# Byte 64 for every stationary operand, byte 0 for every moving one

## The reference

```python
# first block, per layer
px = modulate(rms_norm(x, g1), sh1, sc1) @ w_in        # same for ctx
mix_x = concat([latent_attention(qx, k_all, v_all), fourier_mix(fx),
                chunk_spatial_gate(ux, gvx, v_g, w_s, b_s)]) @ w_out
x = x + gt1 * mix_x
x = x + gt2 * square(relu(modulate(rms_norm(x, g2), sh2, sc2) @ w1)) @ w2
# second block, per layer
proj = rms_norm(x, attn_norm_g) @ w_in_2               # 3656 columns
mix = concat([moba(...), diff(...), dsa(...)])         # three attentions
x = x + mix @ w_out_2
h2 = rms_norm(x, ffn_norm_g)
x = x + (silu(h2 @ w_gate_2) * (h2 @ w_up_2)) @ w_down_2
```

## The kernel before

| stage | stationary | moving | columns | matmuls | stationary byte before | after |
|---|---|---|---|---|---|---|
| rows1, layers 0 and 1 | act | w | 512 / 256 | 432 / 48 | 0 | 64 |
| out1, layers 0 and 1 | act | w | 512 | 288 | 0 | 64 |
| up1, layer 0 | w | act | 512 / 256 | 672 / 192 | 0 | 64 |
| up1, layer 1 | w | act | 256 | 768 | 64 | 64 |
| down of MLP 1, layers 0 and 1 | hid1 | w | 512 | 1152 | 0 | 64 |
| rows2 and out2, both layers | act | w | 512 / 328 / 256 | 768 / 96 / 96 | 0 | 64 |
| up2, both layers | w | act | 256 | 2112 | 64 | 64 |
| down of MLP 2, both layers | hid2 | w | 512 | 528 | 0 | 64 |

## Time and profile before

### The profile page before, as it was taken

The page is one execution under the profiler, slowest core; times in us unless marked ns, Lnnn a source line. Parts: engine busy times, 40 slices in busy tenths (PEclk is TensorE's granted clock), DMA queues, the critical chain, the costliest instruction groups (busy, mean ns, idle before and its releaser), DMA issues.

```text
span 1592.6 us, 23486 instructions
## 1 busy us (share of the span) xinstructions
PE 1541.2 (97%) x9164; PEld 1262.6 (79%) x9164; DVE 1028.4 (65%) x1577; ACT 795.5 (50%) x1356; POOL 114.2 (7%) x130
## 2 busy tenths in 40 slices
PE   6999999999999999998999999999999999999999
PEld 2864689778888887567898878779998787689987
DVE  3637756455456437576785576978995558879973
ACT  3537735343345225565664456645554456555542
POOL 0111000010001000100000031010000111000000
PEclk9999999999999999999999999999999999999999
DMA  9528623487568524586998689436665596356653
GB/s 360 152 84 313 215 75 114 145 264 253 162 220 277 162 66 133 176 279 190 335 319 300 211 272 312 160 108 183 191 197 191 184 326 227 106 141 192 198 190 115
DMA packets 201005, 322.41 MB, mean 202 GB/s; under 512 B 14576, under 2 KB 100864, under 8 KB 200768
## 3 DMA queue, kind: packets, MB, share of 16 engines
q1 hardware_dynamic: 192992, 293.51, 57.6%
q0 software_dynamic: 7680, 27.34, 4.8%
q10 hardware_dynamic: 224, 0.07, 0.0%
HBM read 298.27 MB, written 22.61 MB: 201 GB/s over the span
## 4 chain that ended last, share of the span: by engine, by line
PE 86%; DVE 7%; DMA 3%; ACT 2%; issue 1%; POOL 0%; SPq 0%; POOLq 0%; DVEq 0%; ACTq 0%
PE bank L2220 53%; PE pair_bank L2220 21%; PE bank L2289 2%; DVE w_lo L1581 1%; PE bank L2537 1%; PE pair_bank L2506 1%; DMA raw<-in_w_in 1%; PE bank L2517 1%; DMA raw<-in_w_ada 1%; PE bank L2315 1%; PE pair_bank L2557 1%; DMA raw<-in_w_mlp 1%; PE bank L2425 0%; PE bank L2571 0%; ACT w_hi L1175 0%
## 5 line engine op out<-in xcount | busy, mean ns | idle before, releaser
L1581 DVE TENSOR_TENSOR w_lo<-raw,w_hi 128x1024 fp32r<-128x1024 f32 (+2 forms) x374 | 447.4, 1218 | 273.5 <-ACT w_hi L1175 272.0
L1175 ACT CAST w_hi<-raw 128x1024 fp32r<-128x1024 f32 (+1 forms) x416 | 428.4, 1045 | 363.2 <-PE bank L2220 236.6
L2220 PE MATMUL pair_bank<-act_hi,w_hi 128*128 128x256 f32 (+1 forms) x744 | 226.8, 305 | 5.0 <-DVE act_lo L1745 2.1
L2220 PE MATMUL pair_bank<-act_hi,w_lo 128*128 128x256 f32 (+1 forms) x744 | 224.7, 302 | 0.0
L2220 PE MATMUL pair_bank<-act_lo,w_hi 128*128 128x256 f32 (+1 forms) x744 | 224.6, 302 | 0.0
L2220 PE MATMUL bank<-w_hi,hid_hi 128*128 128x512 f32 x560 | 220.2, 393 | 0.0
L2220 PE MATMUL bank<-w_lo,hid_hi 128*128 128x512 f32 x560 | 219.6, 392 | 0.0
L2220 PE MATMUL bank<-w_hi,hid_lo 128*128 128x512 f32 x560 | 219.4, 392 | 0.0
L2220 PE MATMUL bank<-w_hi,act_hi 128*128 128x512 f32 (+2 forms) x528 | 206.6, 391 | 8.4 <-DVE w_lo L1581 4.0
L2220 PE MATMUL bank<-w_hi,act_lo 128*128 128x512 f32 (+2 forms) x528 | 200.3, 379 | 0.0
L2220 PE MATMUL bank<-w_lo,act_hi 128*128 128x512 f32 (+2 forms) x528 | 200.1, 379 | 0.0
(11 more groups left out here) (249 smaller groups left out, 2088.9 us busy)
## 6 DMA issues: line engine op xcount, KB each, us to landing
raw<-in_w_mlp SPq DMA_DIRECT2D x128, 512.0 KB, 4.9
raw<-in_w_in SPq DMA_DIRECT2D x112, 512.0 KB, 4.5
raw<-in_w_ada SPq DMA_DIRECT2D x96, 512.0 KB, 5.6
raw<-in_w_gate SPq DMA_DIRECT2D x44, 512.0 KB, 3.8
raw<-in_w_up SPq DMA_DIRECT2D x44, 512.0 KB, 3.8
raw<-in_w_down SPq DMA_DIRECT2D x44, 512.0 KB, 3.6
split_lo<-w_lo POOLq DMA_DIRECT2D x36, 512.0 KB, 5.0
w_lo<-split_lo SPq DMA_DIRECT2D x36, 512.0 KB, 5.1
```

What stands on the lines that cost most here:

```text
L1175: nc.scalar.copy(hi_of(i)[:, 0:w], raw_of(i)[:, 0:w]).then_inc(hi_ready, 1)
L1581: nc.vector.tensor_tensor(lo_of(i)[:, 0:w], raw_of(i)[:, 0:w], hi_of(i)[:, 0:w].bitcast(F32), ALU.subtract).then_inc(lo_ready, 1)
L2220: ins = nc.tensor.matmul(o, a[x], b[y], start=first and i == 0, stop=True, skip_group_check=True)
```

## The change

The activations get rooms that are 32 floats wider, [128, 8, 544], with two views each: view 0 starts at float 16 (byte 64), view 1 at float 0. What is written for an even m, and the mixed heads, goes to view 0, where they are stationary; what is written for an odd m goes to view 1, where they move. Slots of first MLP products, now all put as `"up"`, start at byte 64, those of layer 0 of the first block too. Pads of 64 bytes put `hid1` and `hid2` at byte 64 (and `wide`, which lies over `hid1_lo`, with them), and pads of 64 bytes put the scratch behind them back. Everything above the rooms lies 2048 bytes higher. Apart from line numbers and the names of the rooms, the rows of every engine's program and the semaphores that each waits for are the same, in the same order.

```diff
-        act_hi = sb("act_hi", [P, KT, 2 * NT], F32R)
-        act_lo = sb("act_lo", [P, KT, 2 * NT], F32R)
+        act_hi_room = sb("act_hi_room", [P, KT, 2 * NT + 32], F32R)
+        act_lo_room = sb("act_lo_room", [P, KT, 2 * NT + 32], F32R)
+
+        def act_views(room):
+            return [room[:, :, at_:at_ + 2 * NT] for at_ in (16, 0)]
+
+        act_hi, act_lo = act_views(act_hi_room), act_views(act_lo_room)
...
+                pad("pad_hid1", 64, s2)
                 hid1_hi = sb("hid1_hi", [P, 16 * 2 * NT], F32R, s2)
                 hid1_lo = sb("hid1_lo", [P, 16 * 2 * NT], F32R, s2)
+                pad("pad_fa1", 64, s2)
                 fa1 = sb("fa1", [P, 2, 2 * NT], F32, s2)
...
+                pad("pad_wide", 64, s2)
                 wide = sb("wide", [P, 4, NT], F32, s2)
...
+                pad("pad_hid2", 64, s2)
                 hid2_hi = sb("hid2_hi", [P, FF2 // P, NT], F32R, s2)
                 hid2_lo = sb("hid2_lo", [P, FF2 // P, NT], F32R, s2)
+                pad("pad_fa2", 64, s2)
...
-            return 16 if i < len(n.slots) and n.slots[i][0] == "narrow" else 0
+            return 16 if i < len(n.slots) and n.slots[i][0] == "up" else 0
...
-                        self.put("narrow" if l else "w", 1024, lambda r: [(tiles(r, 4), src[:, 4 * q:4 * q + 4, c:c + 256])])
+                        self.put("up", 1024, lambda r: [(tiles(r, 4), src[:, 4 * q:4 * q + 4, c:c + 256])])
...
-                nc.scalar.copy(act_hi[:, 4 * a:4 * a + 4, NT + t * P:NT + (t + 1) * P], tiles(turned_bank(m, t, a)[:], 4)).then_inc(norm_hi, 1)
+                nc.scalar.copy(act_hi[m % 2][:, 4 * a:4 * a + 4, NT + t * P:NT + (t + 1) * P], tiles(turned_bank(m, t, a)[:], 4)).then_inc(norm_hi, 1)
...
-                nc.scalar.copy(act_hi[:, k:k + 2, c:c + NT], tiles(b, 2)).then_inc(mix_hi, 1)
+                nc.scalar.copy(act_hi[0][:, k:k + 2, c:c + NT], tiles(b, 2)).then_inc(mix_hi, 1)
...
-                return [a[:, k, g * P:(g + 1) * P] for a in (act_hi, act_lo)]
+                return [a[:, k, g * P:(g + 1) * P] for a in (act_hi[0], act_lo[0])]
...
-                                ins = self.three(o, [v[:, kk, f * P:(f + 1) * P] for v in w], [a[:, k, c0:2 * NT] for a in (act_hi, act_lo)],
+                                ins = self.three(o, [v[:, kk, f * P:(f + 1) * P] for v in w], [a[:, k, c0:2 * NT] for a in (act_hi[1], act_lo[1])],
```

More of the change, by code:

```diff
@@ L959, in up2 @@
                         for q in range(2):
-                            self.put("narrow", 1024, lambda r: [(tiles(r, 4), src[:, 4 * q:4 * q + 4, j * 256:(j + 1) * 256])])
+                            self.put("up", 1024, lambda r: [(tiles(r, 4), src[:, 4 * q:4 * q + 4, j * 256:(j + 1) * 256])])
             def finish(self):
@@ L1231, in norm_part @@
                         wait_wide(self.e, m, s, k)
-                        nc.scalar.copy(act_hi[:, k, s * NT:(s + 1) * NT], wide_at(m, s, k)).then_inc(norm_hi, 1)
+                        nc.scalar.copy(act_hi[m % 2][:, k, s * NT:(s + 1) * NT], wide_at(m, s, k)).then_inc(norm_hi, 1)
                         n.put("norm_hi", (m, s, k))
@@ L1245, in context_part @@
                     wait_wide(self.e, m, CTX, k + 1)
-                    nc.scalar.copy(act_hi[:, k:k + 2, 0:NT], wide[:, k % 4:k % 4 + 2, :]).then_inc(norm_hi, 1)
+                    nc.scalar.copy(act_hi[m % 2][:, k:k + 2, 0:NT], wide[:, k % 4:k % 4 + 2, :]).then_inc(norm_hi, 1)
                     n.put("norm_hi", (m, CTX, k + 1))
@@ L1402, in out_ @@
                 self.e.wait_ge(mixed, n.at("mixed", (st["key"], j)))
-                nc.scalar.copy(act_hi[:, k:k + 2, c:c + NT], tiles(bank[b][:], 2)).then_inc(mix_hi, 1)
+                nc.scalar.copy(act_hi[0][:, k:k + 2, c:c + NT], tiles(bank[b][:], 2)).then_inc(mix_hi, 1)
                 n.put("mix_hi", (st["key"], st["group"]))
@@ L1455, in diff_turn @@
                 self.e.wait_ge(mix_full, n.at("mix_full", ("diff", l, t)))
-                nc.scalar.mul(act_hi[:, 2 + 2 * t:4 + 2 * t, 0:NT], tiles(bank[7][:], 2), sub_g[:, l:l + 1]).then_inc(mix_hi, 1)
+                nc.scalar.mul(act_hi[0][:, 2 + 2 * t:4 + 2 * t, 0:NT], tiles(bank[7][:], 2), sub_g[:, l:l + 1]).then_inc(mix_hi, 1)
                 n.put("mix_hi", ("diff", l, t))
@@ L1667, in low @@
                     e.wait_ge(norm_hi, n.at("norm_hi", (m, CTX, k + 1)))
-                    nc.vector.tensor_tensor(act_lo[:, k:k + 2, 0:NT], wide[:, k % 4:k % 4 + 2, :], act_hi[:, k:k + 2, 0:NT].bitcast(F32),
+                    nc.vector.tensor_tensor(act_lo[m % 2][:, k:k + 2, 0:NT], wide[:, k % 4:k % 4 + 2, :], act_hi[m % 2][:, k:k + 2, 0:NT].bitcast(F32),
                                             ALU.subtract).then_inc(norm_lo, 1)
@@ L1693, in low @@
                         e.wait_ge(norm_hi, n.at("norm_hi", (m, s, k)))
-                        nc.vector.tensor_tensor(act_lo[:, k, s * NT:(s + 1) * NT], wide_at(m, s, k),
-                                                act_hi[:, k, s * NT:(s + 1) * NT].bitcast(F32), ALU.subtract).then_inc(norm_lo, 1)
+                        nc.vector.tensor_tensor(act_lo[m % 2][:, k, s * NT:(s + 1) * NT], wide_at(m, s, k),
+                                                act_hi[m % 2][:, k, s * NT:(s + 1) * NT].bitcast(F32), ALU.subtract).then_inc(norm_lo, 1)
                         n.put("norm_lo", (m, s, k))
@@ L1744, in norm_low @@
                 at_ = slice(4 * a, 4 * a + 4), slice(NT + t * P, NT + (t + 1) * P)
-                nc.vector.tensor_tensor(act_lo[:, at_[0], at_[1]], tiles(turned_bank(m, t, a)[:], 4), act_hi[:, at_[0], at_[1]].bitcast(F32),
+                nc.vector.tensor_tensor(act_lo[m % 2][:, at_[0], at_[1]], tiles(turned_bank(m, t, a)[:], 4), act_hi[m % 2][:, at_[0], at_[1]].bitcast(F32),
                                         ALU.subtract).then_inc(norm_lo, 1)
@@ L1927, in mix_low @@
                 self.e.wait_ge(mix_hi, n.at("mix_hi", key))
-                nc.vector.tensor_tensor(act_lo[:, k:k + 2, c:c + NT], tiles(b, 2), act_hi[:, k:k + 2, c:c + NT].bitcast(F32),
+                nc.vector.tensor_tensor(act_lo[0][:, k:k + 2, c:c + NT], tiles(b, 2), act_hi[0][:, k:k + 2, c:c + NT].bitcast(F32),
                                         ALU.subtract).then_inc(mix_lo, 1)
@@ L2080, in diff_turn @@
                 c = slice(2 + 2 * t, 4 + 2 * t)
-                nc.vector.scalar_tensor_tensor(act_lo[:, c, 0:NT], tiles(bank[7][:], 2), sub_g[:, l:l + 1], act_hi[:, c, 0:NT].bitcast(F32),
+                nc.vector.scalar_tensor_tensor(act_lo[0][:, c, 0:NT], tiles(bank[7][:], 2), sub_g[:, l:l + 1], act_hi[0][:, c, 0:NT].bitcast(F32),
                                                ALU.mult, ALU.subtract).then_inc(mix_lo, 1)
@@ L2716, in up1_open @@
                                 ins = self.three(up1_bank(0, 0, idx)[:, s * NT:(s + 1) * NT], [v[:, kk, f * P:(f + 1) * P] for v in w],
-                                                 [a[:, k, s * NT:(s + 1) * NT] for a in (act_hi, act_lo)], (s, k) == (CTX, 0))
+                                                 [a[:, k, s * NT:(s + 1) * NT] for a in (act_hi[1], act_lo[1])], (s, k) == (CTX, 0))
                                 if s == X and k == KT - 1 and f == 0:
@@ L2848, in up2 @@
                                     ins = self.three(b[:, f * NT:(f + 1) * NT], [v[:, kk, f * P:(f + 1) * P] for v in w],
-                                                     [a[:, k, NT:2 * NT] for a in (act_hi, act_lo)], k == 0 and f == 0)
+                                                     [a[:, k, NT:2 * NT] for a in (act_hi[1], act_lo[1])], k == 0 and f == 0)
                             self.took(ins, ("up2", l, j, which) if q == 1 else None)
```

## The result

The changed kernel takes 1604.95 us (median of 4 runs, 1603.65 to 1607.11) against 1592.3 us (4 runs, 1591.66 to 1597.04). The ratio on record is 1.0068 (95% interval 1.0052 to 1.0083): slower, where 1571 was forecast. The profiled execution of the changed kernel took 1603.65 us, span 1601.8, against 1594.35 and 1592.6.

The account below looks back on a forecast made before the run. TensorE, busy 97% of the 1592.6 us span, bounds the kernel, the three-product helper being 74% of the chain. Gains of 25.8 us less 2.9 and 1.0 leave 21.9, giving 1572.5 or 1570.1; predicted 1571, range 1550 to 1596.

Parts of the forecast that it names:

- The other 2880, all 256 wide, have it at byte 64 already.: Count of 7152 helper matmuls: 2880 in the narrow stages already have their stationary operand at byte 64, so no gain counted.
- The edits cost nothing else that I can find: End of the sum: same instruction order and semaphores, splits as fast, DMA difference covered; no cost charged.
- The price at 512 columns, 6.1 ns: Main term: 3840 matmuls 512 wide each gain 6.1 ns from byte 64, 229.9 to 223.8 ns, 23.4 us.
- the effect ends at 256: Rival, chance 0.25: wider streams cover the weight load, only 2.0 us gained; 1593 by the profile, 1591 by the median.
- the 328-wide products that do not care about byte 64: Contrary sign in the 328-wide block: products moving from byte 0, 32 and 64 all take 150 ns each.
- one pair of rows at 256: 256-wide paces before: 119.4 ns at byte 0 (first MLP), 113.3 at byte 64; read as 6.1 ns a matmul.
- a weight load takes 188 ns at both widths: Ground for moving the 256-wide price to 512: equal load time, so the saving is 6.1 ns per load, not per column.
- The price at 256 columns: Term for 336 matmuls 256 wide, 192 of them in the first MLP: 6.1 ns each, 2.0 us.
- The rival "slower": Rival, chance 0.13: the shift puts 512-wide matmuls at the slow place, 234.2 ns; 1609 at worst, about 1602 if half.
- The ports: Skill's rule of two independent SBUF read ports: no start byte could matter, time would stay at about 1594.
- The half that I took off for waits in the attention stages: Deduction for the second block's two attention stages: half of their 5.7 us gain lost in waits, −2.9 us.

Follow-up runs that it names:

- The step alone: Kernel before with its two activation tensors 32 floats wider and nothing else, no operand moved modulo 128: 1603.29 us, 1.0062.
- with the step mended: Changed kernel with activation rooms 64 instead of 32 floats wider than the tokens, pieces 2304 bytes apart: 1596.58 us, 1.0020 to the kernel before.
- the kernel with slots of 4352 bytes: Kernel before with weight slots 1088 instead of 1056 floats apart and 128-byte pads: 1588.97 us, 0.9964; once more for a second profile, 1588.4 us.
- the one-line edit of `up1`: Kernel before with byte 64 also given to weight slots of the first MLP's first layer, activation step still 2048: 1594.03 us, 1.0000.

## Why the prediction was wrong

**"The other 2880, all 256 wide, have it at byte 64 already."** This step lost the sign. I counted a matmul as untouched when its stationary byte stayed, and let the room's new width pass under "The edits cost nothing else that I can find", a term of nothing that measured about 10 us. The width moved the start of the moving operand modulo 256 in the very stages that had the fast pace. The step alone costs 0.62%, the whole change 0.68%; with the step mended 0.20% is left. The trace of before could not have priced it, since no narrow stage of it had such a start, but comparing addresses only modulo 128, as my stage table does, hid the question.

**The price at 512 columns, 6.1 ns.** This term, 23.4 us of the sum, is nothing with weights stationary (232.7 ns, where 226.4 was forecast) and 0.5 to 1.6 ns the other way with hidden activations stationary. No run moved the 1488 matmuls alone that have the activations stationary; with the step mended their starts lie 231.3 ns apart on the mean, against 230.5 before. The 328-wide ones stay at 149 to 151 ns. The rival "the effect ends at 256" had this part right, and the earlier trace rows, the 328-wide products that do not care about byte 64, were its sign; I let one pair of rows at 256 outweigh them on the ground that a weight load takes 188 ns at both widths. That a saving is per load and so the same at every width was an assumption, and it failed.

**The price at 256 columns** held: 5.8 ns instead of 6.1 when taken away (11.44 against 10.88 us a piece). Where a kernel gives it to new matmuls it is not certain: of the three opening pieces of `up1` one fell only to 117.9.

**The rival "slower"** named the right range, 1602 to 1609, by the wrong mechanism: it let the 512-wide pieces all fall to the slow place. The long ones moved by 1.7 ns at most; most of the loss was elsewhere. That 1604.95 lies in its range is luck. Its ground, that pieces of 2.72 and 2.81 us show a place beyond 128 bytes, was sound, and led to the kernel with slots of 4352 bytes, where all long pieces run at 226.8.

**The ports.** From the Trainium skill's rule of two independent read ports ("TensorE: Matmul & The Clock Gate", step-by-step part) I read that no start byte could matter, and set the pair 119.4 and 113.3 against it. The runs side with the pair: the same products take 113.3, 117.1, 117.8 or 119.2 ns at 256 columns when only the places of operands are changed. Whether the ports have a part in it was not measured, and why a narrow stage keeps 117.8 although its moving starts are alike, as in the second `up2` of both profiles with slots of 4352 bytes, stays open.

The half that I took off for waits in the attention stages was not tested, since no gain at 512 columns came from the change. (The pads of the diff are five, not the four that I counted.)

## What to carry over

When a buffer is padded to move a start address, compare the start of every access before and after at more than one power of two, for the operand that was not meant to move above all; a row step that is no multiple of 256 bytes changed the place of one and cost more than the move gave. A price measured at one matmul width is a price at that width: one slot kind moved alone (the one-line edit of `up1`) would have shown it. The pace of a merged piece of the chain, its length by its count, is sharp to 0.1 ns for pieces of 96 here and tells such paces apart at once. And matmuls that become slower cost nothing where the chain waits for a transfer anyway: the stage with that wait showed 0.2 of 2.9 us.

## What was not expected of the hardware

The two `up2` stages of the first kernel with slots of 4352 bytes, busy time by stretch:

```profile
core 0: us, PE busy (x) PEld busy (x) DVE busy (x) ACT busy (x) POOL busy (x), PEclk, DMA share, GB/s
1066.80:1186.70 119.90, 119.90 (x1057) 119.90 (x1058) 109.17 (x88) 62.83 (x77) 0.00 (x0) 1.00 0.65 192
1397.70:1522.20 124.50, 124.50 (x1057) 124.50 (x1058) 109.37 (x89) 62.66 (x77) 0.00 (x0) 1.00 0.62 182
```

The second is 4.6 us longer at the same granted clock of 1.00, with TensorE busy throughout and the same work on VectorE and ScalarE. So a stage of 1056 narrow matmuls can keep a slower pace from its second piece to its end at places modulo 256 at which another keeps the fast one. Three paces were seen at 256 columns: 113.3 ns, some 117 to 118 (117.1 with a moving step of 2176 bytes, 117.8 with high and low 128 bytes apart), and 119.2 with every stationary operand at byte 0 modulo 128. At 512 columns the same place modulo 256 for stationary and moving operands gives an even 226.8 ns in the long `down` pieces, against 229.6 to 230.3 where slots alternate.
